# The router of a mixture-of-experts step on unscaled residual rows, with the norm's scale in its weights

## What is computed

```python
    x = x + gate1 * m
    h = rms_norm(x, g_ffn) * (1.0 + scale2) + shift2
    x = x + gate2 * expert_choice_ffn(h, *moe_w)

    cap = CAPACITY_FACTOR * n // N_EXPERTS
    aff = jax.nn.softmax(jnp.einsum('bnd,de->bne', h, w_router).astype(jnp.float32), axis=-1)
    gates, idx = lax.top_k(jnp.swapaxes(aff, 1, 2), cap)
```

## Time and profile before

| | |
|---|---|
| median of 3 runs | 1391.89 us (1390.16 to 1393.05) |
| the profiled execution's own time | 1392.58 us |
| its span in the trace | 1390.9 us |
| busy share PE / DVE / ACT / POOL | 89% / 70% / 54% / 10% |
| granted TensorE clock, mean | 0.959 |
| DMA, mean over the span | 212 GB/s |

### The profile page before, as it was taken

How to read it: one execution, slowest core, us unless ns; L and a number is a source line. 1 busy time by engine, 2 the same in 40 slices (tenths; PEclk the granted TensorE clock), 3 DMA queues, 4 the chain that set the end, 5 groups by cost and what they waited for, 6 DMA issues and landing times.

```text
span 1390.9 us, 17364 instructions
## 1 busy us (share of the span) xinstructions
PE 1233.0 (89%) x5946; PEld 970.6 (70%) x5946; DVE 978.3 (70%) x1246; ACT 749.1 (54%) x1040; POOL 134.5 (10%) x203
## 2 busy tenths in 40 slices
PE   2789988888889999998449999999999999999982
PEld 0568766667767777776248888778887888778861
DVE  1744527788756332444389999899999999799956
ACT  1522225666633221223428886688866887678831
POOL 2131430000000000000701000100010000200002
PEclk9899988999999999999769999999999999999996
DMA  8642221111053344554219997899968997999911
GB/s 327 249 146 68 84 69 38 39 30 29 1 212 121 122 121 141 213 196 188 113 38 367 381 371 285 293 338 378 365 233 299 386 361 300 344 345 381 369 74 75
DMA packets 109480, 295.24 MB, mean 212 GB/s; under 512 B 29857, under 2 KB 31602, under 8 KB 108642
## 3 DMA queue, kind: packets, MB, share of 16 engines
q1 hardware_dynamic: 102802, 265.99, 52.7%
q0 software_dynamic: 6032, 19.43, 4.2%
q10 hardware_dynamic: 576, 8.91, 1.6%
HBM read 276.78 MB, written 12.27 MB: 208 GB/s over the span
## 4 chain that ended last, share of the span: by engine, by line
PE 76%; DVE 12%; ACT 3%; DMA 3%; issue 3%; POOL 1%; SPq 1%; DVEq 0%; ACTq 0%; POOLq 0%
PE ps L1044 12%; PE ps L1045 12%; PE ps L1046 11%; PE ps L663 9%; PE ps L664 8%; PE ps L665 8%; PE ps L836 2%; PE ps L852 2%; DVE neg_max L1632 2%; DVE raw_lo L1722 2%; DMA raw<-in_w_mod_dram 2%; DMA raw<-in_w_exp_up_dram 1%; PE ps L875 1%; PE ps L685 1%; PE ps L871 1%
## 5 line engine op out<-in xcount | busy, mean ns | idle before, releaser
L1722 DVE TENSOR_TENSOR raw_lo<-raw,w_hi 128x1024 fp32r<-128x1024 f32 x256 | 300.9, 1217 | 29.0 <-ACT w_hi L1368 26.7
L1368 ACT ACTIVATE w_hi<-raw 128x1024 fp32r<-128x1024 f32 x252 | 259.2, 1058 | 61.8 <-PE ps L1046 58.0
L1044 PE MATMUL ps<-w_hi,xe_hi 128*128 128x512 f32 x512 | 207.2, 405 | 1.8 <-DVE xe_lo L1886 1.8
L1046 PE MATMUL ps<-w_hi,xe_lo 128*128 128x512 f32 x512 | 201.3, 393 | 0.0
L1368 ACT ACTIVATE w_hi<-extra 128x1024 fp32r<-128x1024 f32 x128 | 135.8, 1064 | 50.2 <-PE ps L1046 42.3
L1722 DVE TENSOR_TENSOR extra_lo<-extra,w_hi 128x1024 fp32r<-128x1024 f32 x128 | 151.9, 1218 | 9.3 <-ACT w_hi L1368 9.1
L663 PE MATMUL ps<-w_hi,ht_hi 128*128 128x512 f32 (+1 forms) x360 | 142.0, 394 | 12.1 <-DVE raw_lo L486 6.4
L664 PE MATMUL ps<-raw_lo,ht_hi 128*128 128x512 f32 (+1 forms) x360 | 139.3, 387 | 0.0
L665 PE MATMUL ps<-w_hi,ht_lo 128*128 128x512 f32 (+1 forms) x360 | 139.2, 387 | 0.0
L486 DVE TENSOR_TENSOR raw_lo<-raw,w_hi 128x1024 fp32r<-128x1024 f32 x50 | 59.9, 1222 | 98.3 <-ACT w_hi L481 97.8
L481 ACT ACTIVATE w_hi<-raw 128x1024 fp32r<-128x1024 f32 x50 | 50.7, 1055 | 133.6 <-DMA raw<-in_w_in_dram 54.3
(11 more groups left out here) (290 smaller groups left out, 2196.4 us busy)
## 6 DMA issues: line engine op xcount, KB each, us to landing
raw<-in_w_exp_down_dram SPq DMA_DIRECT2D x112, 512.0 KB, 5.2
raw<-in_w_exp_gate_dram SPq DMA_DIRECT2D x80, 512.0 KB, 5.4
extra<-in_w_exp_up_dram SPq DMA_DIRECT2D x64, 512.0 KB, 5.7
raw<-in_w_exp_up_dram SPq DMA_DIRECT2D x64, 512.0 KB, 6.0
raw<-in_w_mod_dram SPq DMA_DIRECT2D x24, 1024.0 KB, 8.5
extra<-in_w_exp_gate_dram SPq DMA_DIRECT2D x48, 512.0 KB, 5.3
raw<-in_w_in_dram SPq DMA_DIRECT2D x17, 1024.0 KB, 5.4
extra<-in_w_exp_down_dram SPq DMA_DIRECT2D x16, 512.0 KB, 5.1
```

Of the source, the lines that this page charges most:

```text
L1044: pe.matmul(b, stat_hi, hi[:, cols], start=(k == 0), stop=False)
L1046: mm = pe.matmul(b, stat_lo, hi[:, cols], start=False, stop=(k == KD - 1))
L1368: act.activation(w_hi[:, (DENSE_SPLITS + h) % NHL, :], expert_half(h), ACT.Copy)\
L1722: dve.tensor_tensor(expert_lo_half(h), expert_half(h), w_hi[:, (DENSE_SPLITS + h) % NHL, :].bitcast(F32), ALU.subtract).then_inc(s_lo, 1)
```

## The change

The router works on `x_r` itself. Its transposes (`turn_rows`) are the x_r columns of `out0` for the first five of ten units, placed before the five tiles of (j=14, hh=2), and those of `out1` for the last five, behind the out product. ACT (nine units, `rows_turned`) and DVE (the last one) only copy them to `x2_t`. The scale goes into the router weights (`router_s`), the shift through them into a vector of 16 (`router_b` against ones, the event "bias" at (14, 1, 2)), and `rs` multiplies the logits at the end. `route` makes, for each tile, eight products of 32 output rows: k and k+4 add up in quadrant k mod 4. A product with `sum_q` (the identity's columns summed over the quadrants) adds the four quadrants and turns the result at the same time. The squares are summed by column half. `xn_f` and `xn_hi` are both made on ACT, behind the Exp. Slot numbers run from 1, which removes the subtraction at the end of step 6, and the first round of `max` reads `aff_t`, which removes a copy. POOL's order and SP's waits change, and the expert halves are split earlier in `out1`. DVE has the same `half_ahead` edit as ACT, and in (14, 1, 2) two small reductions and two copies of at most 64 columns.

```diff
-         (14, 0, 2): ("spread", 10, 0), (14, 0, 4): ("spread", 10, 1), (14, 2, 3): ("spread", 11, 0),
+         (14, 0, 2): ("spread", 10, 0), (14, 0, 4): ("spread", 10, 1), (14, 1, 2): ("bias", 0), (14, 2, 3): ("spread", 11, 0),
...
-    t[:, T_IOTA:T_IOTA + 64] = np.arange(64)
+    t[:, T_IOTA:T_IOTA + 64] = 1 + np.arange(64)
...
-                        sp.wait_ge(s_x2t, KD)
-                        sp.wait_ge(s_xh, NT)
+                        sp.wait_ge(s_lgt, 2)
+                    elif h == 2 * NRAW + 2:
                         sp.wait_ge(s_xl, NT)
-                    elif h == 2 * NRAW + 2:
-                        sp.wait_ge(s_lgn, 1)
-                        sp.wait_ge(s_pos, 1)
...
+                if event[0] == "bias":
+                    pe.wait_ge(s_rt, 4)
+                    pe.matmul(bank(6, 0, 2 * KD * NE), ones_m[:, :], router_b[:, :, :, :].rearrange("p v k e -> p (v k e)"),
+                              start=True, stop=True).then_inc(s_post, 1)
...
+            def turn_rows(n):
+                hh, t = n // NT, n % NT
+                pe.wait_ge(s_x1 if hh else s_x0, t + 1)
+                if n == 0:
+                    pe.wait_ge(s_free_d, freed_before("dve", NT * 14 - 1))
+                elif n < NT:
+                    pe.wait_ge(s_x2e, n)
+                elif n == NT:
+                    pe.wait_ge(s_mod, MODS_DONE)
+                else:
+                    pe.wait_ge(s_x2e, n - 1)
+                for i in range(4):
+                    k = 4 * hh + i
+                    mm = pe.transpose(bank(row_bank(n), i * P, (i + 1) * P), x_r[:, t, k * P:(k + 1) * P], ident)
+                mm.then_inc(s_x2t, 1)
+            def route(t):
+                if t == NT - 1:
+                    pe.wait_ge(s_x2d, 1)
+                else:
+                    pe.wait_ge(s_x2e, NT + t + 1)
+                if t == 0:
+                    pe.wait_ge(s_row, 12)
+                for k in range(KD):
+                    q = 32 * (k % 4)
+                    mm = pe.matmul(bank(7, t * P, (t + 1) * P, slice(q, q + 32)) if t < NTL else bank(5, 0, P, slice(q, q + 32)),
+                                   router_s[:, t // NTL, k, :], x2_t[:, k, t * P:(t + 1) * P], start=(k < 4), stop=(k >= 4))
+                if t >= NTL - 1:
+                    mm.then_inc(s_lgt, 1)
...
+                    if j == 14 and hh == 2:
+                        turn_rows(t)
...
-            pe.wait_ge(s_free_d, freed_before("dve", NT * 15 - 1))
-            for k in range(KD):
-                if k == 0:
-                    pe.wait_ge(s_xf, NT)
-                if k >= 3:
-                    pe.wait_ge(s_h2, k - 2)
-                for t in range(NTL):
-                    pe.transpose(bank(2 * (k % 3), t * P, (t + 1) * P), xn_f[:, t, k * P:(k + 1) * P], ident)
-                pe.transpose(bank(2 * (k % 3) + 1, 0, P),
-                             xn_f[:, NTL, k * P:(k + 1) * P], ident).then_inc(s_x2t, 1)
-            pe.wait_ge(s_router, 16)
-            for k in range(KD):
-                pe.wait_ge(s_h2, k + 1)
-                pe.matmul(bank(6, rows=e16), router[:, k, :], h2_t[:, k, 0:LAT], start=(k == 0), stop=(k == KD - 1))
-                mm = pe.matmul(bank(7, 0, CTX, rows=e16), router[:, k, :], h2_t[:, k, LAT:TOK],
-                               start=(k == 0), stop=(k == KD - 1))
+            for n in range(NT, 2 * NT):
+                turn_rows(n)
+                if n > NT:
+                    route(n - NT - 1)
+            route(NT - 1)
+            pe.wait_ge(s_x2e, 2 * NT)
+            for t in range(NT):
+                if t == NT - 1:
+                    pe.wait_ge(s_x2d, 2)
+                mm = pe.matmul(bank(4, t * NE, (t + 1) * NE), lg_t[:, t, :], sum_q[:, :], start=True, stop=True)
             mm.then_inc(s_lgt, 1)
-            pe.wait_ge(s_lgc, 1)
-            for t in range(NT):
-                mm = pe.transpose(bank(0, t * NE, (t + 1) * NE), lg_t[:, t * P:(t + 1) * P], ident[0:NE, 0:NE])
-            mm.then_inc(s_lgn, 1)
...
+            def squares_of(v, t):
+                act.wait_ge(s_x1 if v else s_x0, t + 1)
+                if v or t:
+                    act.wait_ge(s_ss2, NT * v + t)
+                act.activation(squares_h[:, :], x_r[:, t, v * NW:(v + 1) * NW], ACT.Square,
+                               accum_out=ss_half[:, v, t:t + 1]).then_inc(s_ss2, 1)
+            def rows_turned(n):
+                hh, t = n // NT, n % NT
+                act.wait_ge(s_x2t, n + 1)
+                act.activation(x2_t[:, 4 * hh:4 * hh + 4, t * P:(t + 1) * P],
+                               bank(row_bank(n)).rearrange("p (k c) -> p k c", c=P), ACT.Copy).then_inc(s_x2e, 1)
...
+                        if j == 14 and hh == 2:
+                            rows_turned(t)
+                        if t == (2, 0)[hh % 2] and (j, hh) != (14, 3):
                             half_ahead(SPLIT_OF[gemm_half(j, hh)] + 2)
-                        if (j, hh) == (14, 3) and t in (1, 3):
-                            half_ahead(DENSE_SPLITS + 2 + t // 2)
+                        if (j, hh) == (14, 2) and t in (3, 4):
+                            half_ahead(DENSE_SPLITS + t - 2)
+                        if (j, hh) == (14, 3) and t == 0:
+                            half_ahead(DENSE_SPLITS + 3)
+                        if (j, hh) == (14, 3):
+                            squares_of(0, t)
...
             act.wait_ge(s_mod, MODS_DONE)
             act.dma_start(g2_dram[:, :, :], gate2[:, :, :]).then_inc(s_g2out, 16)
             for t in range(NT):
-                act.wait_ge(s_x1, t + 1)
-                if t:
-                    act.wait_ge(s_ss2, t)
-                act.activation(squares2[:, :], x_r[:, t, :], ACT.Square, accum_out=ss[:, t:t + 1]).then_inc(s_ss2, 1)
+                squares_of(1, t)
+                if t < NT - 1:
+                    rows_turned(NT + t)
+            act.wait_ge(s_lgt, 1)
+            act.activation(lg_t[:, 0:NTL, :], bank(7).rearrange("p (t c) -> p t c", c=P), ACT.Copy).then_inc(s_x2e, 1)
             act.dma_start(x1_dram[:, :, :], x_r[:, :, :]).then_inc(s_x1out, 16)
+            act.wait_ge(s_sub, 1)
+            act.activation(soft[:, :, :], soft[:, :, :], ACT.Exp).then_inc(s_sexp, 1)
             act.wait_ge(s_g2out, 16)
-            for t in range(NT):
+            act.wait_ge(s_rs2, 1)
+            for t in range(NT):
+                act.activation(xn_f[:, t, :], x_r[:, t, :], ACT.Identity, scale=rs[:, t:t + 1]).then_inc(s_xf, 1)
                 act.wait_ge(s_xf, t + 1)
                 act.activation(xn_hi[:, t, :], xn_f[:, t, :], ACT.Copy).then_inc(s_xh, 1)
-            for k in range(KD):
-                act.wait_ge(s_x2t, k + 1)
-                act.activation(h2_t[:, k, 0:LAT], bank(2 * (k % 3)), ACT.Identity, scale=scale2[:, k, 0:1],
-                               bias=mod_t[:, 24 + k, 0:1])
-                act.activation(h2_t[:, k, LAT:TOK], bank(2 * (k % 3) + 1, 0, P), ACT.Identity,
-                               scale=scale2[:, k, 1:2], bias=mod_t[:, 24 + k, 1:2]).then_inc(s_h2, 1)
-            act.wait_ge(s_sub, 1)
-            act.activation(soft[:, :, :], soft[:, :, :], ACT.Exp).then_inc(s_sexp, 1)
...
+            dve.wait_ge(s_x2t, 2 * NT)
+            dve.tensor_copy(x2_t[:, 4:8, NTL * P:TOK], bank(row_bank(2 * NT - 1)).rearrange("p (k c) -> p k c", c=P))\
+               .then_inc(s_x2d, 1)
+            dve.memset(ones16[:, :], 1.0).then_inc(s_dve, 1)
+            dve.wait_ge(s_dve, own())
+            dve.wait_ge(s_lgt, 2)
+            dve.tensor_copy(lg_t[:, NTL, :], bank(5, 0, P)).then_inc(s_x2d, 1)
+            logits = bank(4, 0, NT * NE).rearrange("p (t e) -> p t e", e=NE)
             dve.wait_ge(s_rs2, 1)
-            for t in range(NT):
-                dve.tensor_scalar(xn_f[:, t, :], x_r[:, t, :], rs[:, t:t + 1], None, ALU.mult).then_inc(s_xf, 1)
-            dve.wait_ge(s_xf, NT)
...
+            dve.wait_ge(s_lgt, 3)
+            dve.tensor_tensor(soft[:, :, :], logits, rs[:, :].unsqueeze(2).broadcast_to([P, NT, NE]), ALU.mult)\
+               .then_inc(s_dve, 1)
             dve.wait_ge(s_dve, own())
+            dve.tensor_tensor(soft[:, :, :], soft[:, :, :], bias_n[:, :, :], ALU.add).then_inc(s_dve, 1)
+            dve.wait_ge(s_dve, own())
...
-            dve.tensor_reduce(soft_s[:, 0, :], logits, AX.X, ALU.max).then_inc(s_dve, 1)
...
-            dve.memset(ones16[:, :], 1.0).then_inc(s_dve, 1)
-            dve.tensor_copy(left[:, :], aff_t[:, :]).then_inc(s_dve, 1)
-            dve.wait_ge(s_dve, own(2))
...
-            dve.tensor_tensor(count[:, :], count[:, :], chosen[:, :], ALU.mult).then_inc(s_dve, 1)
-            dve.wait_ge(s_dve, own())
-            dve.tensor_scalar(pos_t[:, :], count[:, :], -1.0, None, ALU.add).then_inc(s_pos, 1)
+            dve.tensor_tensor(pos_t[:, :], count[:, :], chosen[:, :], ALU.mult).then_inc(s_pos, 1)
...
-            pool.wait_ge(s_half, DENSE_HALVES)
```

(53 more changed lines are left out.)

55 lines of the change are left out of this document (31 added, 24 removed).

## The result

| | before | change |
|---|---|---|
| median (range), 4 runs each | 1391.48 us (1390.16 to 1393.05) | 1369.24 us (1367.55 to 1370.90) |
| the profiled execution's own time / span | 1392.58 / 1390.9 | 1370.90 / 1368.9 |
| `mod_keep` copy in (14, 1) to the first expert product | 85.92 us | 62.15 us |
| the first expert product to the end of the span | 663.84 us | 666.35 us |

The change is faster: ratio 0.9841, 95% interval 0.9829 to 0.9852, that is 22.2 us.

What follows compares the result with a forecast made beforehand. PE is 89% busy; a serial 70.1 us stage before the expert products was taken as the target. Minus 20.8 to the first `max`, minus 0.5 subtraction, plus 1.8 hold: minus 19.5 us, median 1372.4, range 1369.5 to 1377.5.

Steps and rivals of the forecast that it cites:

- the expert stage starts as much sooner as the stage is shorter: PE is busy behind the router stage, so shortening that stage should move the end by the same amount.
- the quadrants run side by side: In `route`, four router products run at once; two rounds of 128 columns take about 0.55 us a tile.
- the rounds are not slowed by POOL: The ten `max` rounds stay at 13.32 us beside POOL; the rival of held rounds had 0.06 (1384) plus 0.02 (1394.2).
- the path behind the out product: From 661.0, ACT alternates four copies and four half squares until 667.1, as the path; `rs` follows at 669.1.
- the length of the hold of `chosen`: After the rounds, `chosen` is due at 686.3 and waits for POOL's memset until about 688.1: plus 1.8, between 0 and 2.9.
- five times four transposes, 0.60 each time: Inside the out product, on a full PE, none hidden; with the 0.43 product, 3.4 us together, ending about 660.3.
- Quadrants in a row: Rival 1, behind the out product: serial quadrants cost 2.3 us, about 1375, or 1377.5 with the clock; chance 0.22 jointly.
- That rival's other half, the clock: Rival 1: PE at half clock costs `route`, `sum_q` and transposes about 2.5 us more, about 1375; joint chance 0.22.
- 661 to 672: Stretch from out product to softmax and transposes; a clock under 0.9 there was named as a sign of rival 1, chance 0.22.
- The first `max`: Start of the ten rounds, forecast at 673.0 instead of 693.80: minus 20.8 us.
- 16.5 us as before: The gather, from the end of `pos_t` to the first expert product, stays unchanged at 16.5 us.
- its 664 us: The expert stage keeps its length; one longer than 664 us was named as a sign of being wrong.

Runs made afterwards that it cites:

- One quadrant: The change, but all eight router products of a tile accumulate in one quadrant, with copy and sum product on 32 rows; stage 68.59 us, median 1375.35 us.
- DVE's two copies: The change, but DVE copies the last two turned units (8 and 9) and ACT one fewer; stage 62.15 us, median 1371.07 us.
- the run with idle products: The change plus 8 unread products ahead of the transposes of `aff_n` and 64 behind them; stage 62.15 us, median 1368.93 us.
- the tail alone: Before, with slots counted from 1, the copy into `left` removed and the memset of ones moved ahead of the logits wait; stage 83.35 us, median 1389.14 us.
- the unscaled rows: Before, with router transposes reading `x_r`, the norm's factor left out of the logits, row splits and POOL's memsets as in the change; stage 78.95 us, median 1384.32 us.
- the version with `acc` first: The change, with POOL's memset of `acc` moved ahead of the two of `xe`; stage 64.69 us, median 1371.93 us.

## Why the prediction was right and wrong

The direction and most of the mechanism were right: the expert stage starts as much sooner as the stage is shorter, the quadrants run side by side, the rounds are not slowed by POOL, and `chosen` is held by a memset. Two things failed: the path behind the out product, which I put on ACT at 1.52 us a tile and which ran on PE at 1.16, and the length of the hold of `chosen`, 1.8 forecast and 0.21 measured. The other sizes were off as well, nearly all to the same side. Times of the change are with 1.17 added.

- *"five times four transposes, 0.60 each time"*: 0.44 each. The row I used stood amid other products, with PE busy ahead of it and behind it, and the chain of the same trace gives that very group 0.44. I took a shown duration, which overlaps its neighbour's, for a price. The last out product ended at 659.5, not 660.3.
- *"This is the path ... 661.0 + 4 x 0.65 + 4 x 0.87 = 667.1"*: the wrong engine and the wrong pitch, and the largest miss ahead of the rounds. ACT's pair takes 1.11 (three quarters of what I counted), so its last square ended at 664.5. The path is PE's own chain, which I had put into ACT's shade; it ended at 666.9 where I had 669.0, and `rs` came at 666.4, not 669.1. One quadrant and DVE's two copies show both halves of it. I had added shown durations of neighbours on one engine as if they never overlapped.
- *Quadrants in a row would cost "2 x 1.15"*: 5.65, for the same reason. That rival's other half, the clock, came true in part: 1.00 from 661 to 666 of the change's trace, where PE's short bursts are and where I had put its risk, but 0.50 at the transposes of `aff_n`, 0.53 us too long by the run with idle products. Over what I had called 661 to 672 (659.8 to 670.8 of the change's trace) the clock was 0.85, under the 0.9 that I had named as a sign of being wrong. That was a loss that the forecast itself left out.
- The first `max`: 671.3 for a forecast of 673.0.
- *`chosen`: "so it waits until about 688.1: plus 1.8"*: 0.21. The rule was right: wherever `chosen` or `pos_t` met a memset, it ended 0.34 or 0.35 us after it, in the change and in six variants of it and of before. The meeting point was wrong. Both engines do count from the same Exp, but POOL's subtractions took 11.59 us and not 12.0 to 12.5, and DVE lost 0.5 in the transposes, so `chosen` came 0.34 us before the memset's end and not 1.8. I should have kept the whole span of 0 to 2.9 as likely: a phase between two engines is known no better than the sum of all errors on either side. The SBUF — State Buffer page of the Trainium skill says in "Who interferes with whom" that a DVE instruction with at most one SBUF input, outside the two-port modes, does not contend with GpSimd. By that rule the rounds lose nothing beside POOL, and the trace agrees: 13.32 us in both kernels. The same section lets a DVE operation with two SBUF inputs wait for a GpSimd one that reads SBUF, not for one that only writes; the scans and the product of two inputs took their usual 1.53 and 0.81 beside memsets, which agrees, and no run here has them beside a subtraction. One reading of mine was short there: of the five scalings in before not one but two were held by the subtractions, 2.88 us each.
- *"16.5 us as before"* for the gather: 16.04. It goes with the clock that PE is granted there, from 13.90 at 1.00 to 17.04 at 0.69.
- *The expert stage is "its 664 us"*: 666.35, a loss of 2.5 us and one of the signs that I had named. Up to the last transposes of `h_act`, 605 us into the stage, 0.64 of it has gathered; why stays open (a clock of 0.94 from 480 to 510 us into the stage is a candidate, but the tail alone has it too and lost nothing up to there). Another 1.17 gather up to the first product of the combine step, and there the clock differs, 0.78 for 0.89; the last 0.7 lie behind it. The 30 us from 600 us into the expert stage, of before and of the change:

```profile
1327.06:1357.06 30.00, 22.19 (x83) 16.70 (x81) 16.50 (x18) 8.69 (x10) 0.00 (x0) 0.89 0.03 11
```
```profile
1302.55:1332.55 30.00, 23.20 (x81) 17.83 (x80) 14.54 (x16) 8.78 (x10) 0.00 (x0) 0.78 0.04 18
```

The change with one quadrant has 0.89 there and an expert stage of 664.19 like before's; the one with DVE's two copies has 0.78 and 666.29. Both are the change in all that runs there, so the loss need not come with the change. But it mostly does: the three traces of before and of its variants have 663.84 to 664.67, seven of the eight of the change and its variants 666.03 to 668.50. Why the clock falls sooner in one trace than in another, and whether the change has a part in it, was not settled.

In sum, the stage was 23.8 us shorter (19.9 forecast, with the 0.43 that my landmark leaves out): 1.7 more than forecast up to the first `max`, 1.6 at `chosen`, 0.5 in the gather. Then 2.5 us went back in the expert stage, an error of the opposite sign, which made the miss smaller than its parts. The rest of the 22.0 us between the two spans is the 1.17 us ahead of the stage, less the 0.43 of the bias product. No part of the forecast speaks of those 1.17 us, and they differ from trace to trace; without them the gain would have been 20.8 us, and inside the range. So it is luck that the total came out so near the range's low end, and on which side of it. The errors of the terms are not luck: the stage repeats.

What each part of the change is worth to the first `max`: the tail 1.36 and the unscaled rows 10.86 (with the 4.2 of held scalings in them), each alone on before; the turns beside the out product, the quadrants and the order of the norm make up the other 10.7, of which the quadrants hold 5.65 when they alone are undone.

## What to carry to other kernels

On a full engine, price an added instruction by the distance from one start to the next in a busy stretch of the trace, or by what the chain gives it, not by its shown duration; where two engines alternate, work out both engines' pitch per round, and let the longer one be the path. An operation that is held by another engine's costs what is left of the other one when it arrives, so its price is a range as wide as the holder is long, until the holder is moved out of its way. An engine that runs dry ahead of a short dense stretch can take a low clock into it: here useless products of 2.1 and 17.5 us, in time that PE had nothing for, bought 2.7 us (0.53 in the transposes, 2.14 in the gather).

## What the runs showed of the hardware that I had not expected

- The spread of one kernel's executions can go with the clock: the change's four took 1370.90, 1369.96, 1368.51 and 1367.55 us at a mean granted clock of 0.959, 0.962, 0.963 and 0.965. It is not all of the spread: of before, in the group with the tail alone, one took 1392.93 us at 0.961 and one 1390.83 us at 0.958.
- 0.34 us pass between the end of a POOL memset and the end of a DVE operation of 16x640 that takes 0.48 when free, in every meeting (0.35 in the change). So the held operation takes less time behind the memset than its whole duration when free; why was not looked into. The memset that follows it on POOL is longer in turn, 3.10 instead of 2.87, in the change and in the version with `acc` first.
- Two neighbours on ACT, a copy out of PSUM (0.60) and a square (0.62), start 0.50 apart: the copy's shown duration is 0.10 longer than the distance to the next start.
- With all turns behind the out product, where PE and ACT share a single PSUM bank, PE is idle for 0.78 us each time it is handed over and back.
